# The low part of a branch source on GpSimd: three instructions change engines or places in a hybrid decoder step

## The reference

```python
z = h @ w_in                                    # u,v | h,Bg,Cg | a,g | three gates
ya = chunk_spatial_gate(gelu(ua), layernorm(gelu(va)), w_s, b_s)
yb = bb * causal_dwconv(cb * hb, conv_b)        # 3 taps
conv_out_c = causal_dwconv(ac * sigmoid(gc), conv_c)   # 31 taps
yc = silu(layernorm(conv_out_c + conv_c_b, ln_c_g, ln_c_b))
gates = sigmoid(zg).reshape(bsz, t, 3, d)
merged = gates[0] * (ya @ w_branch[0]) + gates[1] * (yb @ w_branch[1]) + gates[2] * (yc @ w_branch[2])
x = x + gate1 * (merged @ w_out)
```

## Time and profile before

| | |
|---|---|
| median of 3 runs (lowest to highest) | 3940.87 us (3939.57 to 3941.14) |
| span of the profiled execution | 3938.8 us |
| TensorE busy | 3859.3 us, 98% |
| VectorE busy | 2731.5 us, 69% |
| ScalarE busy | 1573.1 us, 40% |
| GpSimd busy | 813.4 us, 21% |
| mean granted TensorE clock | 0.994 of full |

### The profile page before, as it was taken

One profiled execution on the slowest core, in us unless ns is written; L12 is line 12 of the kernel. 1 busy time (PEld: TensorE's weight loads), 2 busy tenths in 40 slices (PEclk: granted clock), 3 DMA queues, 4 the chain that ended last, 5 costly groups with the idle time before them and its releaser, 6 DMA issues.

```text
span 3938.8 us, 76121 instructions
## 1 busy us (share of the span) xinstructions
PE 3859.3 (98%) x29048; PEld 3787.5 (96%) x29048; DVE 2731.5 (69%) x4471; ACT 1573.1 (40%) x2658; POOL 813.4 (21%) x690
## 2 busy tenths in 40 slices
PE   7999999999999999999999999999999999999998
PEld 5999999999999999999989989999999999999998
DVE  4488479777666547787755875897766664587776
ACT  3222333333777633333332233333347774333332
POOL 1000000000222135555200000000002221455551
PEclk9999999999999999999999999999999999999999
DMA  6553423544566679999834423235446667799995
GB/s 232 130 140 132 154 85 96 172 142 138 163 186 194 201 238 349 345 352 349 302 122 104 152 78 118 81 119 164 138 136 182 186 194 217 261 350 347 350 349 192
DMA packets 418219, 781.86 MB, mean 199 GB/s; under 512 B 151184, under 2 KB 274448, under 8 KB 417344
## 3 DMA queue, kind: packets, MB, share of 16 engines
q1 hardware_dynamic: 176640, 441.70, 34.9%
q10 hardware_dynamic: 194240, 196.10, 15.7%
q0 software_dynamic: 47104, 141.00, 10.1%
HBM read 655.79 MB, written 122.88 MB: 198 GB/s over the span
## 4 chain that ended last, share of the span: by engine, by line
PE 91%; DVE 4%; ACT 3%; issue 1%; DMA 1%; ACTq 0%; DVEq 0%; SPq 0%
PE pg L1698 18%; PE pg L1701 18%; PE pg L1705 18%; PE pm L2033 5%; PE pm L2034 5%; PE pm L2035 5%; PE pg L2033 5%; PE pg L2034 5%; PE pg L2035 5%; PE pm L1986 2%; DVE ys L1311 1%; DVE w_lo L1097 1%; ACT one_j L1015 1%; PE pm L1737 1%; PE pm L1951 1%
## 5 line engine op out<-in xcount | busy, mean ns | idle before, releaser
L1097 DVE TENSOR_TENSOR w_lo<-raw,w_hi 128x1024 fp32r<-128x1024 f32 x688 | 841.0, 1224 | 909.2 <-ACT w_hi L990 699.3
L990 ACT CAST w_hi<-raw 128x1024 fp32r<-128x1024 f32 x499 | 524.2, 1051 | 781.3 <-PE pg L2035 734.8
L1698 PE MATMUL pg<-a_hi,w_hi 128*128 128x260 f32 x6272 | 822.3, 283 | 3.4 <-ACT w_hi L691 1.7
L1705 PE MATMUL pg<-a_hi,w_lo 128*128 128x260 f32 x6272 | 814.0, 282 | 0.0
L1701 PE MATMUL pg<-a_lo,w_hi 128*128 128x260 f32 x6272 | 813.8, 282 | 0.0
L1698 PEld LDWEIGHTS pg<-a_hi,w_hi 128*128 128x128 f32 x6272 | 778.3, 188 | 14.6 <-issue 10.9
L1701 PEld LDWEIGHTS pg<-a_lo,w_hi 128*128 128x128 f32 x6272 | 777.1, 188 | 0.0
L1705 PEld LDWEIGHTS pg<-a_hi,w_lo 128*128 128x128 f32 x6272 | 776.9, 188 | 0.0
L649 POOL DMA_INDIRECT rows<-stream,at_v x256 | 281.9, 1101 | 766.4 <-DVE acc_tok L1595 314.4
L659 POOL TENSOR_TENSOR one_j<-one_j,g_lo 128x896 fp32r<-128x896 f32 x112 | 189.8, 1695 | 1041.1 <-ACTq L1018 1041.1
L697 ACT ACTIVATE hid<-pg 128x260 f32<-128x260 f32 x512 | 170.5, 385 | 507.4 <-PE pg L1705 486.1
(11 more groups left out here) (261 smaller groups left out, 5349.0 us busy)
## 6 DMA issues: line engine op xcount, KB each, us to landing
raw<-stream SPq DMA_DIRECT2D x688, 512.0 KB, 4.0
hidden_dram<-hid SPq DMA_DIRECT2D x256, 196.0 KB, 3.5
gate_dram<-gate_buf ACTq DMA_DIRECT2D x28, 1792.0 KB, 10.7
hid_in<-hidden_dram ACTq DMA_DIRECT2D x64, 784.0 KB, 6.0
gate_in<-gate_dram ACTq DMA_DIRECT2D x64, 784.0 KB, 11.1
ada_raw<-stream ACTq DMA_DIRECT2D x64, 512.0 KB, 4.1
hid_tok<-hid SPq DMA_DIRECT2D x256, 64.0 KB, 3.5
ys<-stream ACTq DMA_DIRECT2D x12, 512.0 KB, 5.2
```

The source lines that it names most:

```text
L990: act.copy(ring(True, m % 4), raw[:, m % 4]).then_inc(hi_ready, 1)
L1097: tt(ring(False, s), raw[:, s], ring(True, s).bitcast(F32), ALU.subtract).then_inc(lo_ready, 1)
L1698: pe.matmul(outs[h], w_hi[:, s, k, :], parts[n][h][0], start=n == 0, stop=False)
L1705: mm = pe.matmul(outs[h], w_lo[:, s, k, :], parts[n][h][0], start=False, stop=n == len(ks) - 1)
```

## The change

For the first two sources GpSimd makes the low part, with the same subtraction; VectorE no longer does. For the third source ScalarE makes the high part right behind the swish, at step 1 and no longer at step 2; VectorE still makes its low part at step 2. The taps are dealt out anew: in branch 0, 6 instead of 3 at step 2, 4 instead of 5 at step 3, 1 instead of 2 at steps 10 and 11; in branch 1, 6 instead of 3 at step 2, 5 instead of 6 at step 8, 3 instead of 5 at step 9. The sums per branch, 50 and 45, stay.

```diff
-BR_TAPS = ((6, 6, 3, 5, 2, 2, 6, 6, 6, 4, 2, 2), (6, 6, 3, 5, 1, 1, 6, 6, 6, 5, 0, 0), (0,) * 12)
+BR_TAPS = ((6, 6, 6, 4, 2, 2, 6, 6, 6, 4, 1, 1), (6, 6, 6, 5, 1, 1, 6, 6, 5, 3, 0, 0), (0,) * 12)
@@ GpSimd, behind the DMAs of hc_s
+                for b in range(2):
+                    pool.wait_ge(yhi_ready, l * 3 + (b + 1))
+                    own.link(pool.tensor_tensor(y_lo[:, :, :], ys[:, b, :, :], y_hi[:, :, :].bitcast(F32), ALU.subtract))
+                    pool.sem_inc(y_ready, 1)
                 own.restart()
@@ ScalarE, each step, behind split and ada_after
-                        if step == 2:
+                        if step == 2 and b < 2:
 
                             act.wait_ge(src_ready, l * 3 + (b + 1))
                             own.link(act.copy(y_hi[:, :, :], ys[:, b, :, :]))
@@ ScalarE, b == 2 and step == 1, behind the swish
                             own.settle()
                             act.sem_inc(src_ready, 1)
+                            own.link(act.copy(y_hi[:, :, :], ys[:, 2, :, :]))
+                            act.sem_inc(yhi_ready, 1)
@@ VectorE, each step, behind split and ada_taken
-                        if step == 2:
-                            dve.wait_ge(yhi_ready, l * 3 + (b + 1))
-                            own.link(tt(y_lo[:, :, :], ys[:, b, :, :], y_hi[:, :, :].bitcast(F32), ALU.subtract))
+                        if (b, step) == (2, 2):
+                            dve.wait_ge(yhi_ready, l * 3 + 3)
+                            own.link(tt(y_lo[:, :, :], ys[:, 2, :, :], y_hi[:, :, :].bitcast(F32), ALU.subtract))
                             dve.sem_inc(y_ready, 1)
```

## The result

| | before | after |
|---|---|---|
| median (lowest to highest), 5 runs each | 3940.87 us (3939.57 to 3944.67) | 3951.87 us (3951.65 to 3958.94) |
| span of the profiled execution | 3938.8 us | 3949.9 us |

The changed kernel is slower: ratio 1.0036, 95% interval 1.0025 to 1.0047. That is 11.0 us between the medians and 11.1 us between the spans, where +14.7 us was forecast. 3951.87 lies in the forecast range.

What follows compares the result with a forecast made beforehand. TensorE, busy 98% of the span, was taken as the bound, so only its waits and clock could change the time; 12.9 - 2.5 + 2.75 + 1.5 = +14.7 us on 3940.9 gave 3955.6 us, range 3937 to 3963.

Steps and rivals of the forecast that it cites:

- The hold at steps 2 to 5: Branches 0 and 1, both layers: VectorE's taps wait while GpSimd reads, so step 5 starts later; +12.9 us; chance 0.50.
- the order of the prediction: Branch 0 in first, then second layer, then branch 1 likewise: +2.56, +2.86, +3.66, +3.84 us.
- The step that had no row: VectorE as the second reader waits for GpSimd's whole instruction; assumed from rows showing only GpSimd waiting for VectorE.
- The hold taken: At steps 2 to 5, VectorE held for GpSimd's whole `y_lo` instruction, taken as 4.3 us a place.
- the middle of the two ends: GpSimd's `y_lo` length: 4.3 us, between 3.9 and 4.65 us scaled by columns from a multiply's records.
- GpSimd losing the turn: Rival at steps 2 to 5: GpSimd gets in only behind the sixth tap; 14.9 instead of 12.9, 3957.6 us; chance 0.16.
- TensorE's wait for `y_lo`: Step 4, branch 0, first layer: lasts to about 252.9; two products of 6.0 us then end at 258.9, before the release.
- no hold: Rival at steps 2 to 5: VectorE reads on while GpSimd reads; -0.7 us at first place, 3938 us total; chance 0.22.
- Steps 8 and 9: Branch 1, both layers: fewer taps there remove TensorE's 0.6 and 1.9 us waits for the finished convolution; -2.5 us.
- Branch 2: Both layers: early high part delays table load, sigmoid and VectorE's split, so the `y_lo` wait grows; +2.75 us.
- The clock: Branch stage: TensorE's clock falls after long waits, 1.5 us each; five falls instead of four, +1.5 us.

Runs made afterwards that it cites:

- e4: Changed kernel with two GpSimd zero fills of `y_lo` in place of each subtraction, so GpSimd writes SBUF and reads nothing: 3941.13 us, ratio 0.9997.
- e8: Changed kernel with each of GpSimd's subtractions done twice in a row: 3970.30 us, ratio 1.0071.
- e9: Changed kernel with a plain GpSimd copy of the source to `y_lo` in place of the subtraction, one input read: 3942.74 us, ratio 1.0012.
- e10: Changed kernel with each GpSimd subtraction cut in four pieces of 520 columns: 3950.23 us, ratio 1.0030.
- e3: Changed kernel with the third source's high part back at step 2; GpSimd's low parts and new taps stay: 3954.15 us, ratio 1.0027.
- e2: Kernel before with the third source's high part right behind the swish and its low part ahead of VectorE's split: 3936.08 us, ratio 0.9987.
- e5: Kernel before with three taps of branch 1 moved, one from step 8 and two from step 9, to step 5: 3940.50 us, ratio 0.9997.
- e1: Kernel before with only the third source's high part moved right behind the swish: 3947.51 us, ratio 1.0013.

## Why the prediction was right

It was right in sign, in mechanism and in most of its terms; the sum was 3.6 us too high.

- **The hold at steps 2 to 5.** From one fixed point (the start of VectorE's split at step 2; in the second layer's branch 1 the start of `y_hi`) to the restart of TensorE at step 5, before and after, in the order of the prediction: 12.86 to 15.37, 12.56 to 15.35, 12.36 to 15.94 and 13.03 to 17.02 us, so +2.51, +2.79, +3.58 and +3.99. Together +12.87; +12.92 was forecast. The step that had no row, VectorE as the one that waits, is shown by e4, e8, e9 and e10: a tap with two inputs waits while GpSimd reads, not while it only writes. The hold taken, 4.3 us, was 4.26 (4.09 in the second layer's branch 1). GpSimd's own instruction is longer, 4.64: the middle of the two ends was too low for it and right for the hold, by luck.
- **GpSimd losing the turn** didn't happen. It came in behind the first tap at every place where the taps ran.
- **TensorE's wait for `y_lo`** at step 4 lay inside VectorE's lateness, as worked out, but with less to spare. It was 1.76 us at the first place. The two products behind it took 7.5 us and not 6.0, because the clock fell, and TensorE stood ready 1.3 us ahead of the release, where the prediction had some 3. So they ended 14.05 us behind the fixed point, 1.2 later than step 5 began before; in e3, where no fall came behind this wait, 12.51, which is 0.35 earlier. Even without a hold, then, the low part on GpSimd could have cost up to 1.2 us here, where the rival *no hold* had -0.7: it left out a fall behind this wait.
- **Steps 8 and 9.** -2.5 us forecast; both waits are gone.
- **Branch 2.** +2.75 forecast. From the start of step 2 on TensorE to step 4, 14.02 to 15.32 us and, in the second layer, 14.18 to 15.49: +2.61. The wait wasn't one for `w_hi`, though the list named it; e2 shows it.
- **The clock** is the term that was mis-sized: +1.5 forecast, about -1.5 measured. The waits before step 4, which the prediction had only as cover, came first, and at three of the four places the clock fell behind those: it reads 0.62 from 253.7 to 258.2.

```profile
253.70:258.20 4.50, 4.50 (x25) 4.50 (x26) 4.32 (x6) 0.17 (x1) 0.00 (x0) 0.62 0.02 6
```

A TensorE that runs slower while VectorE is late loses nothing: only the wait behind it gets shorter. e3 has the same place without a fall. Its wait at step 5 is 2.87 us where the changed kernel's is 1.32, and step 5 begins 15.38 us behind the fixed point, against 15.37:

```profile
254.57 1.19 PE L1702 MATMUL pg<-y_hi,w_hi 128*128 128x260 f32 x8 [1.76 <-issue]
...
263.41 1.19 PE L1702 MATMUL pg<-y_hi,w_hi 128*128 128x260 f32 x8 [2.87 <-DVEq L1108]
```

Falls that cost something were three (second layer branch 1, and branch 2 in both), against four before: 12.9 - 2.5 + 2.6 - 1.5 = 11.5, against 11.1 to 11.2 measured. That the number of falls follows the waits is not shown: e5 has one where the kernel before, with the same wait, has none.

Open is why the medians of e1 and e3 stand 3 to 4 us higher than their stages say. The rest of the span, with nothing changed in it, was 5 us longer in their profiled executions, and the mean granted clock of the whole span was 0.992 and 0.991 there, against 0.994 before. What lowers it outside the stage is not shown.

## What to carry to other kernels

Before work moves from VectorE to GpSimd, look at what VectorE does meanwhile. If both read SBUF, and VectorE reads two tensors there, the move costs VectorE nearly all of GpSimd's time: here 4.3 us held to save 2.3. Look too at whoever waits for the result: it came later from GpSimd, and TensorE's wait for it was next in line behind the hold. A result made earlier helps only if its consumer takes it earlier: put the consumer's instruction ahead of the one that waits for the same, now later, producer. And a hand-dealt filler belongs in the steps with idle time behind them; moving the taps there was worth more than taking work off the engine.

## What the runs showed of the hardware

- GpSimd and VectorE exclude each other by whole instructions when GpSimd reads SBUF (one tensor: 1.55 us of hold under 1.96; two: 4.26 under 4.65) and VectorE's instruction has two SBUF inputs. GpSimd's fills of 1.84 us held none of these.
- A VectorE `TENSOR_SCALAR` with one SBUF input (512 columns, 0.55 us alone) was held by both: 1.12 and 2.11 us under fills (e4), 4.67 under a subtraction (e8), 1.40 and 1.38 under its pieces (e10). Why it differs from the two-input taps under a fill no run here shows.
- Subtracting 2080 fp32 columns takes GpSimd 4.64 us, VectorE 2.32. The Trainium skill (GPSIMD Engine Reference, section Performance versus the Vector engine) gives 4497 ns for 2048 columns, by columns an estimate of 4.57 us: the trace agrees within 2%.
- SBUF — State Buffer of the Trainium skill, section Who interferes with whom, states the exclusion of the two engines for reads, and in order of issue. These runs agree: 4.26 us in one tap, 8.44 in two.
